# Twelve modulation slabs of the first stage land in two idle buffers, in pairs between pairs of split slabs

## The reference

```
h    = rmsnorm(x, norm_mix)
proj = h @ w_in                       # (256 x 1024) @ (1024 x 6672)
qa, ka, va, ra, a_lr, qb, kb, vb, gates = split(proj)
log_a = log_sigmoid(a_lr @ w_lr_up + b_forget) / 16
oa = gla_chunked(qa, ka, va, log_a);  oa = oa * rsqrt(mean(oa*oa) + eps) * norm * silu(ra)
ob = moba_attention(qb, kb, vb, rel_bias)          # softmax, a bias by distance
x  = x + (g_a * (oa @ w_a) + g_b * (ob @ w_b)) @ w_out;  x = x + conv_ffn(rmsnorm(x))
# second block, for its two layers i:
mod = silu([c, c_ctx]) @ ada_w[i] + ada_b[i]        # (2 x 1024) @ (1024 x 6144)
# layer 0: conformer convolution and conv-ffn on latent and context tokens, shifted, scaled and gated by mod
# layer 1: window attention with rope and sinks, conv-ffn; then a last rmsnorm
```

## Time and profile before

| | us |
|---|---|
| median of 3 runs | 1374.36 (1373.31 to 1374.72) |
| the profiled execution | 1374.51 |
| its span, first to last instruction | 1372.6 |
| PE busy | 1356.5 (99%) |
| VectorE, ScalarE, GpSimd busy | 1015.3, 855.3, 395.8 |
| chain that ended last, by engine | PE 88%, DVE 6%, DMA 3%, ACT 2%, issue 1% |
| granted TensorE clock, mean | 0.999 |
| DMA | 272.33 MB, mean 198 GB/s |

### The profile page before, as it was taken

How to read it: one execution, slowest core, us unless ns; L and a number is a source line. 1 busy time by engine, 2 the same in 40 slices (tenths; PEclk the granted TensorE clock), 3 DMA queues, 4 the chain that set the end, 5 groups by cost and what they waited for, 6 DMA issues and landing times.

```text
span 1372.6 us, 25276 instructions
## 1 busy us (share of the span) xinstructions
PE 1356.5 (99%) x10118; PEld 1240.8 (90%) x10118; DVE 1015.3 (74%) x1337; ACT 855.3 (62%) x1248; POOL 395.8 (29%) x193
## 2 busy tenths in 40 slices
PE   9999999999999999999999999999999999999997
PEld 7788889999999999899999999999999868888886
DVE  5323664858899998788999989777776696665556
ACT  5433565647888856667898575655555486655554
POOL 2442443243100011231100111666662201143333
PEclk9999999999999999999999999999999999999999
DMA  8776775565244444774333546555554713455551
GB/s 314 277 253 241 268 272 230 180 222 174 105 184 183 184 184 154 290 284 156 153 153 161 228 152 263 220 220 222 219 191 180 268 41 130 184 184 184 183 187 58
DMA packets 39684, 272.33 MB, mean 198 GB/s; under 512 B 4611, under 2 KB 5891, under 8 KB 7084
## 3 DMA queue, kind: packets, MB, share of 16 engines
q1 hardware_dynamic: 39308, 270.57, 52.4%
q10 hardware_dynamic: 288, 0.54, 0.1%
HBM read 270.02 MB, written 1.06 MB: 197 GB/s over the span
## 4 chain that ended last, share of the span: by engine, by line
PE 88%; DVE 6%; DMA 3%; ACT 2%; issue 1%; POOL 0%; DVEq 0%; ACTq 0%; SPq 0%
PE ps L2156 18%; PE ps L2157 17%; PE ps L2158 17%; PE ps L2191 10%; PE ps L780 9%; PE ps L2194 5%; PE ps L2315 3%; DMA raw<-w_dram 2%; PE ps L2206 2%; DVE wlo L1467 1%; PE ps L2216 1%; PE ps L2692 1%; PE ps L2678 1%; ACT whi L966 1%; DVE gates L1645 1%
## 5 line engine op out<-in xcount | busy, mean ns | idle before, releaser
L924 POOL TENSOR_TENSOR wlo<-raw,whi 128x64 fp32r<-128x64 f32 (+1 forms) x185 | 393.7, 2130 | 956.5 <-ACT whi L966 956.2
L1467 DVE TENSOR_TENSOR wlo<-raw,whi 128x1984 fp32r<-128x1984 f32 (+1 forms) x185 | 335.3, 1814 | 235.0 <-ACT whi L966 234.8
L966 ACT ACTIVATE whi<-raw 128x2048 fp32r<-128x2048 f32 x185 | 352.5, 1909 | 239.8 <-DMA raw<-w_dram 133.9
L2156 PE MATMUL ps<-h_both,whi 128*128 128x256 f32 x928 | 268.2, 289 | 0.0
L2157 PE MATMUL ps<-h_both,whi 128*128 128x256 f32 x928 | 262.4, 283 | 0.0
L2158 PE MATMUL ps<-h_both,wlo 128*128 128x256 f32 x928 | 262.4, 283 | 0.0
L2156 PE MATMUL ps<-g_both,whi 128*128 128x256 f32 x752 | 217.0, 289 | 0.0
L2157 PE MATMUL ps<-g_both,whi 128*128 128x256 f32 x752 | 212.7, 283 | 0.0
L2158 PE MATMUL ps<-g_both,wlo 128*128 128x256 f32 x752 | 212.7, 283 | 0.0
L2156 PEld LDWEIGHTS ps<-h_both,whi 128*128 128x128 f32 x928 | 177.7, 191 | 8.5 <-issue 7.6
L2157 PEld LDWEIGHTS ps<-h_both,whi 128*128 128x128 f32 x928 | 177.8, 192 | 0.5
(11 more groups left out here) (334 smaller groups left out, 2464.8 us busy)
## 6 DMA issues: line engine op xcount, KB each, us to landing
raw<-w_dram SPq DMA_DIRECT2D x243, 1024.0 KB, 4.8
sra<-w_dram SPq DMA_DIRECT2D x2, 1024.0 KB, 5.9
mqk<-w_dram SPq DMA_DIRECT2D x2, 1024.0 KB, 5.8
brev<-w_dram SPq DMA_DIRECT2D x2, 1024.0 KB, 6.9
gates<-w_dram SPq DMA_DIRECT2D x2, 1024.0 KB, 8.6
brev<-w_first_keys_dram SPq DMA_DIRECT2D x1, 1024.0 KB, 7.7
brev<-bias_rows SPq DMA_DIRECT2D x1, 1024.0 KB, 9.0
brev<-ctxT_dram SPq DMA_DIRECT2D x1, 1024.0 KB, 8.1
```

What stands on the lines that cost most here:

```text
L924: pool.tensor_tensor(wlo[:, g.slot, part], raw[:, g.slot, part], whi[:, g.slot, part].bitcast(F32), ALU.subtract).then_inc(lo2_done, 1)
L966: act.activation(whi[:, g.slot, :], raw[:, g.slot, :], ACT.Copy).then_inc(hi_done, 1)
L1467: dve.tensor_tensor(wlo[:, g.slot, part], raw[:, g.slot, part], whi[:, g.slot, part].bitcast(F32), ALU.subtract)\
L2156: pe.matmul(out, w[0], x[0], start=start, stop=False, skip_group_check=True)
```

## The change

The load of twelve modulation slabs (ada 1 to 12) leaves the ring. They land in two buffers that are idle at that time: the odd ones in `brev` (after the first keys are used, before the distance bias lands there), the even ones in `sra` (after the table matmul, before silu(ra) goes there). PE's order takes them in pairs: ada 0, mix 2, ada 1, ada 2, mix 3, mix 4, ada 3, ada 4, mix 5, mix 6 and so on to mix 14; from ada 13 on the order is as before. Up to mix 14 the ring holds mixer slabs alone (and ada 0). ScalarE and VectorE split at each item up to `split_ahead(n)`: two ring items ahead instead of three, none at mix 2, three from ada 13 on. SyncE loads an early slab once the slab before in the same buffer is used. Besides, the small columns and the two halves of x change between SyncE's and ScalarE's queue, PE warms up with 14 matmuls, GpSimd's mask stands two ring items earlier, and before the attention of layer 1 VectorE takes one slab's remainder in the middle of `scale` instead of behind it.

```diff
-for _g in range(2, N_MIX):
+MOST = 6
+WARMING = 14
+ASIDE_ADA = range(1, 13)
+LEAD = [("ada", 0), ("mix", 2)]
+for _g in range(3, 15, 2):
+    LEAD += [("ada", _g - 2), ("ada", _g - 1), ("mix", _g), ("mix", _g + 1)]
+for _g in range(15, N_MIX):
     if _g - 2 < N_ADA:
         LEAD.append(("ada", _g - 2))
     LEAD.append(("mix", _g))
+def early(kind, i):
+    return kind == "ada" and i in ASIDE_ADA
+IN_RING = [item for item in LEAD if not early(*item)]
+TURN = {item: n for n, item in enumerate(IN_RING)}
+def split_ahead(n):
+    return 2 if n == 1 else n + 2 if n <= TURN["mix", 14] else n + 3
...
+        early_slab = [flat(sra[:, :, :]), flat(brev[:, :, :])]
...
+            def load_early(i):
+                if i == 1:
+                    sp.wait_ge(keys_done, 1)
+                elif i == 2:
+                    sp.wait_ge(tab_done, 1)
+                else:
+                    sp.wait_ge(early_done, i - 2)
+                sp.dma_start(early_slab[i % 2], io["w"][STORE["early"][0] + i - 1]).then_inc(early_landed[i % 2], 16)
...
+                    load_early(1)
+                    load_early(2)
+                    run(c, name, first, 3, 5)
+                    run(c, name, first, 5, 6)
+                    for i in range(3, 11, 2):
+                        load_early(i)
+                        load_early(i + 1)
+                        if i == 3:
+                            sp.wait_ge(tab_sb, 1)
+                            sp.dma_start(io["scratch"], flat(state[0:H_MOBA, 0, 0:2, :])).then_inc(tab_out, 16)
+                        run(c, name, first, i + 3, i + 5)
...
-            for n, (kind, g) in enumerate(LEAD):
+            ahead = 3
+            for kind, g in LEAD:
...
+                if early(kind, g):
+                    continue
...
-                hi(Slab(n + RING))
+                while ahead <= split_ahead(TURN[kind, g]):
+                    hi(Slab(ahead))
+                    ahead += 1
...
                 for t in range(KT):
+                    if between and t == KT // 2:
+                        between()
...
-            scale(8, xlat, gain_of(5), bufA)
-            c = lo_to(c, "qkv", 1)
+            scale(8, xlat, gain_of(5), bufA, between=lambda: lo_to(c, "qkv", 1))
```

More of the change, by code:

```diff
@@ L82, with group_ended @@
     LEAD.append(("mix", _g))
-TURN = {item: n for n, item in enumerate(LEAD)}
+def early(kind, i):
[4 more added lines that the diff above has]
+    return 2 if n == 1 else n + 2 if n <= TURN["mix", 14] else n + 3
+def group_ended(n):
+    if LEAD[n][0] == "mix":
+        for kind, i in LEAD[max(n - 2, 0):n][::-1]:
+            if kind == "mix":
+                break
+            if i % MOST == MOST - 1:
+                return i
+    return None
 def lead_stream():
-    out, rest = [], list(LEAD)
+    out, rest = [], list(IN_RING)
     while rest:
@@ L121 @@
 RUN_ORDER = [
-    ("lead", "lead", 0, len(LEAD)), ("gla", "gla", 0, 4), ("moba", "moba", 0, 2),
+    ("lead", "lead", 0, len(STREAM)), ("gla", "gla", 0, 4), ("moba", "moba", 0, 2),
     ("pw1_ctx_a", "pw1", 0, 2), ("out", "out", 0, 4), ("pw1_ctx_b", "pw1", 2, 6),
@@ L151, in stored @@
 def stored():
-    at, n = {"ada1": N_ADA}, 0
+    at, n = {"ada1": N_ADA, "early": len(ASIDE_ADA)}, 0
     for _, name, first, k in RUN_ORDER:
@@ L457, in build @@
                                                         sem("window_out_hi"), sem("window_out_lo"))
+        early_landed, early_done = [sem("early_landed0"), sem("early_landed1")], sem("early_used")
         lower_sb, joined = sem("lower_sums_copied"), sem("sums_joined")
@@ L836, in run @@
                     load(name, first + k, Slab(c + k))
+            def load_early(i):
[6 more added lines that the diff above has]
+                sp.dma_start(early_slab[i % 2], io["w"][STORE["early"][0] + i - 1]).then_inc(early_landed[i % 2], 16)
             def load_aside(use, k):
                 sp.dma_start(aside[ASIDE_AT[use][k]], io["w"][STORE["ada1"][0] + GROUP_SLABS[use][0] + k]).then_inc(aside_landed, 16)
-            sp.dma_start(xlat[:, 0:KT // 2, :], io["xT"][:, 0:KT // 2, :]).then_inc(s_x[0], 16)
+            first = COL["cond"][0] + 2 * KT
+            sp.dma_start(cols[:, 0:first], io["cols"][:, 0:first]).then_inc(s_first, 16)
+            sp.dma_start(xlat[:, KT // 2:KT, :], io["xT"][:, KT // 2:KT, :]).then_inc(s_x[1], 16)
             sp.dma_start(lr_down, io["w_lr_down"]).then_inc(s_lr, 16)
@@ L851, in _ @@
                     sp.dma_start(wlr, io["w_lr_up"]).then_inc(s_small, 16)
-                    run(c, name, first, 2, RING)
+                    run(c, name, first, 2, 3)
                     rest = COL["cond"][0] + 2 * KT
@@ L855, in _ @@
                     sp.dma_start(consts[:, :, :], io["consts"]).then_inc(s_consts, 16)
[L856 to L860, removed]
+                    load_early(1)
[9 more added lines that the diff above has]
+                        run(c, name, first, i + 3, i + 5)
+                    load_early(11)
+                    load_early(12)
+                    run(c, name, first, AT["mix", 15], AT["mix", 16])
+                    run(c, name, first, AT["mix", 16], AT["mix", 16] + 1)
                     sp.wait_ge(tab_out, 16)
-                    sp.wait_ge(keys_done, 1)
+                    sp.wait_ge(early_done, 11)
                     sp.dma_start(brev[:, :, :], bass.AP(io["scratch"].tensor, 0, [[1, P], [512, H_MOBA], [1, T]]))\
                       .then_inc(brev_in, 16)
-                    run(c, name, first, 8 * RING + 2, count)
+                    run(c, name, first, AT["mix", 16] + 1, count)
                     sp.wait_ge(sub_done, 3)
@@ L937, in run @@
                     lo(Slab(c + k))
-            masked_at = AT["mix", 8] + RING + 2
-            run(0, "lead", 0, masked_at)
+            masked_at = AT["mix", 8] + RING
+            run(0, "lead", 0, 1)
+            run(0, "lead", 1, masked_at)
             attn = bufA[:, 0:1024].rearrange("p (a i) -> p a i", i=P)
@@ L947, in _ @@
             pool.memset(attn[0:CHUNK, :, CHUNK:P], 0.0).then_inc(attn_masked, 1)
-            run(0, "lead", masked_at, len(LEAD))
-            c = len(LEAD)
+            run(0, "lead", masked_at, len(STREAM))
+            c = len(STREAM)
             for use, _, _, count in RUN_ORDER[1:]:
@@ L995, in split_hi, with mod_rows @@
                         between(t // 2)
-            def mod_rows(i, g):
+            def mod_rows(i):
                 q = i // MOST
-                act.wait_ge(slab_done, g + 1)
+                if early("ada", i):
+                    act.wait_ge(early_done, i)
+                else:
+                    act.wait_ge(slab_done, TURN["ada", i] + 1)
                 if q >= 2:
@@ L1095, in gate_bias @@
                 ins.then_inc(xb_done, 1)
-            first = COL["cond"][0] + 2 * KT
-            act.dma_start(cols[:, 0:first], io["cols"][:, 0:first]).then_inc(s_first, 16)
-            act.dma_start(xlat[:, KT // 2:KT, :], io["xT"][:, KT // 2:KT, :]).then_inc(s_x[1], 16)
+            act.dma_start(xlat[:, 0:KT // 2, :], io["xT"][:, 0:KT // 2, :]).then_inc(s_x[0], 16)
             act.wait_ge(s_memset, 2)
@@ L1130, in exponentials @@
                 act.activation(state[:, 0, :, :], state[:, 0, :, :], ACT.Exp).then_inc(e_done, 1)
-            for n, (kind, g) in enumerate(LEAD):
+            ahead = 3
+            for kind, g in LEAD:
                 if kind == "ada" and g % MOST == MOST - 1:
-                    mod_rows(g, n)
+                    mod_rows(g)
+                if early(kind, g):
+                    continue
                 if (kind, g) == ("ada", LAST_ROUND):
                     exponentials(2)
-                hi(Slab(n + RING))
+                while ahead <= split_ahead(TURN[kind, g]):
+                    hi(Slab(ahead))
+                    ahead += 1
                 if kind == "ada":
                     continue
-                act.wait_ge(slab_done, n + 1)
+                act.wait_ge(slab_done, TURN[kind, g] + 1)
                 if g < 3:
@@ L1158, in _ @@
                     if g == 15:
-                        act.wait_ge(tab_done, 1)
+                        act.wait_ge(early_done, len(ASIDE_ADA))
                     drain(g, sra[:, 2 * (g - 15):2 * (g - 15) + 2, :], ACT.Silu)
@@ L1477, in fold, with scale @@
                 dve.tensor_tensor(sq[:, 0:512], sq[:, 0:512], sq[:, 1024:1536], ALU.add).then_inc(fold_done, 1)
-            def scale(n, x, gains, y, first=None):
+            def scale(n, x, gains, y, first=None, between=None):
                 dve.wait_ge(std_done, n + 1)
@@ L1772, in _ @@
                     normalise(2)
-                lo(Slab(n + RING))
-                was, i = LEAD[n - 1] if n else ("", 0)
-                if was == "ada" and i % MOST == MOST - 1:
+                while ahead <= split_ahead(TURN[kind, g]):
+                    lo(Slab(ahead))
+                    ahead += 1
+                i = group_ended(n)
+                if i is not None:
```

(9 more changed lines are left out.)

7 lines of the change are left out of this document (2 added, 5 removed).

## The result

| | before | after |
|---|---|---|
| median of 6 runs, us | 1374.20 (1373.31 to 1375.19) | 1383.62 (1381.19 to 1385.28) |
| the profiled execution | 1374.51 | 1384.42 |
| its span | 1372.6 | 1382.7 |
| PE busy | 1356.5 | 1357.0 |
| granted TensorE clock, mean | 0.999 | 0.994 |

The ratio is 1.0067, 95% interval [1.0056, 1.0078]. The kernel after was timed once more beside other kernels: 1383.31 us against 1374.43, ratio 1.0067 [1.0053, 1.008]. The forecast was 1379.9, in a range of 1376.6 to 1382.2: the direction is right, the size is not, and the time lies outside the range.

A forecast was written before the change was run, and what follows sets the result against it. PE was taken as the bound, busy 1356.5 of 1372.6 us. Terms -1.4 + 3.5 - 0.7 + 4.9 - 0.8 = +5.5 us gave 1379.9 us, range 1376.6 to 1382.2.

The forecast's parts named there:

- The new waits: First stage: PE waits for late splits, 3.5 us at mix 4 and 4.9 us at mix 16.
- The new wait is 3.5 us: At mix 4: its split stands behind mix 2's drain, Abs, Exp and Ln; +3.5 us, bounds 3.2 and 4.0.
- The wait is 4.9 us: At mix 16: VectorE's remainder follows reciprocal, product and GpSimd's part; +4.9 us, bounds 2.7 and 5.3.
- the choice of 4.9 against 2.7: At mix 16: 4.9 us if GpSimd's part holds up VectorE's remainder, 2.7 if the two merely run side by side.
- The waits that go: First stage: the wait for mix 6's drain goes, -0.7 us, and the wait at mix 18's turn shrinks, -0.8.
- the changes of work: PE's first stage: pairing slabs means fewer changes of work; -1.4 us, bounds -2.0 and -0.5.
- Startup: Kernel start: changed load queues and two fewer warm-up matmuls give 0 us, bounds -1.5 and +0.5.
- The edit before the attention: Before the attention's projections: +1.0 us for a new wait, -0.9 for a landing; 0, bounds -0.9 and +1.2.
- rival 2: GpSimd's parts end sooner than their spans: waits of 1.2 at mix 4, 2.7 at mix 16; 1375.4 us, chance 0.06.
- Rival 3: At mix 16, a late slab makes GpSimd's part miss the product: wait 2.7, not 4.9; 1377.7 us, chance 0.11.
- Rival 4: Loads become late in SyncE's in-order queue; one late landing costs PE about +2: 1381.9 us, chance 0.09.
- Rival 1: At mix 4 and mix 16 the splits keep ahead, no new waits: -2.9, 1371.5 us, chance 0.05.

The follow-up runs named there:

- Experiments 1: Kernel after, with the split of mix 16 taken earlier, ahead of ScalarE's square root and VectorE's reciprocal: 1377.81 us.
- 2: Kernel after, with the split of mix 4 taken earlier and its load issued ahead of the second early slab: 1377.88 us.
- 6: Kernel after with mix 4 and mix 16 both split earlier: 1371.90 us; on top, the attention edit undone: 1372.24, or the old startup: 1371.92.
- experiment 5: Kernel after, with one more wait on GpSimd: its part of mix 17 begins after VectorE's remainder of mix 16: 1381.14 us.
- Experiments 3: Kernel after, with matmuls on ones ahead of mix 4 (14) and mix 16 (21), keeping PE busy in both waits: 1379.85 us.
- 4: Kernel before, with PE made to wait at mix 16 for mix 17's remainder: bare 1381.29 us, filled with 26 matmuls on ones 1379.33 (nine runs each).
- the repaired kernel: Kernel after with the splits of mix 4 and mix 16 both taken earlier: 1371.90 us, and 1372.72 us when timed again as yardstick.
- the filled one: Kernel after, with 14 matmuls on ones ahead of mix 4 and 21 ahead of mix 16: 1379.85 us.

## Why the prediction was right in kind and wrong in size

- **The new waits**: right in place, cause and length (3.41 for 3.5, 5.07 for 4.9). Experiments 1, 2 and 6 show that they are what makes the kernel slower: with both splits earlier it is faster than before. That GpSimd's part falls between product and remainder, the choice of 4.9 against 2.7, is shown by experiment 5. The Trainium skill ("SBUF — State Buffer", section "Who interferes with whom") has the rule that a VectorE instruction with two SBUF inputs contends with a GpSimd one that reads SBUF, and the trace agrees: 4.50 against 2.35 us.
- **The step that failed** is "The new wait is 3.5 us" and "The wait is 4.9 us", read as the cost. They were added to the sum at their own length. The granted clock was noted as 1.00 in the earlier trace rows and taken for granted, but that was the clock of a PE that waited for nothing longer than 1.2 us there. The waits took it to its lower level, and the slabs behind them ran slowly: +3.2 in the profile. The forecast with it is +8.7, against +9.4 and +8.9 measured. Experiments 3 and 4 show it from both sides: idleness filled, the slabs are fast; idleness put into the old kernel, its slab is slow and costs 2.0 us of time. The Trainium skill ("TensorE: Matmul & The Clock Gate", section "Part 1: The HAM clock gate") has the rule that idleness lowers the clock and work raises it again, and that how many matmuls run slowly differs from run to run; the traces agree, 7.05, 7.31, 7.32 and 8.36 us for the same slab behind the same 3.4 us. It would have belonged in the sum.
- **The waits that go and the changes of work**: right in the profile of the kernel after (-0.8, -0.8, -1.6 for -0.7, -0.8, -1.4), though the -1.6 is what the other rows leave and was not measured by itself. In the version with both splits only two of the three hold. The wait at mix 18's turn is back there at 1.20 us, and one of 0.35 is new near 182 us; the drain's 0.8, some 1.8 for the changes of work (again what is left) and 0.3 at the start, less that new wait, make its first stage end 2.6 us earlier than before.
- **Startup** gave 0.5 in the profile, inside its bounds (experiment 6); no time shows it. **The edit before the attention** did what was worked out (+1.1, -1.1); the 0.8 behind it differs from profile to profile, down to nothing.
- **The rivals**: rival 2 falls (it had waits of 1.2 and 2.7, measured are 3.4 and 5.1; in experiment 5 GpSimd's span is real enough to hold VectorE up). Rival 3's 2.7 is what a GpSimd that stays out gives, 2.9. Rival 4 fell short: no landing kept PE waiting in the first stage of the kernel after, and none for more than 0.8 us behind it. Rival 1 was not the case, but its sum comes near the repaired kernel: -2.9 worked out, -2.7 and -2.1 measured. That is partly luck, as its -0.8 for mix 18's turn is not in that kernel.
- **The range** took its ends from the bounds of each term, and no term had the clock. An unnamed term widens no range.

## What to carry to other kernels

Where PE has been busy without a break, price a new wait at its length and a slow stretch behind it, here 1.2 to 2.5 us for waits of 2.9 to 5.8 us, and look at the clock of the stretch, not only at the wait. When buffers let work be reordered, check what the in-order engines that feed it now do first: two splits taken a few places earlier were worth the whole loss and turned it into a gain. Matmuls on nothing in an unavoidable wait can pay.

## What the runs showed of the hardware that was not expected

The fall of the clock can come after the wait is over: in experiment 5 PE had been back at work for 0.4 us behind a wait of 3.4, and for 0.8 us behind one of 2.9, when its matmuls became slow. The cost of the slow stretch hardly follows the length of the wait: +1.5 us behind 2.9 (7.41 for 5.95), +1.2, +1.5, +1.5 and +2.5 behind the same 3.4, +1.6 to +2.3 behind 5.1, +2.3 and +2.4 behind 5.8 and 5.6. And the kernel after spreads more (1381.2 to 1385.3) than the one before beside it (1373.3 to 1375.2) or the filled one (1379.5 to 1380.3), which fits a cost that differs from run to run. The mean granted clock of each run points the same way: the fastest run of the kernel after (1381.19 us) has 0.996, the slowest (1385.28) 0.994, and the fastest run of the kernel with the split of mix 16 earlier (1375.74) has 0.998, as the kernel before has, while its profiled one (1377.21) has 0.995. That the clock is the cause of the spread was not tried, and the kernel before also had one run of 1378.14 us at 0.997.
